# Modulation rows by column-tiled TensorE products, and two side steps per place in the hybrid stage

## What is computed

```python
def adaln(c, w, b):
    mod = jax.nn.silu(c) @ w + b                 # c: 1 x 1024, w: 1024 x 3072
    shift, scale, gate = jnp.split(mod[:, None, :], 3, axis=-1)
    return shift, scale, gate

def modulate(x, norm_w, shift, scale):
    return rmsnorm(x, norm_w) * (1 + scale) + shift

# for each of hyb, dense, ssm, moe:
shift, scale, gate = adaln(c, mod_w, mod_b)
x = x + gate * stage(modulate(x, norm, shift, scale))
```

## Time and profile before

| | |
|---|---|
| median of three runs | 2512.43 us (2510.99 to 2514.09) |
| the profiled execution, its own time | 2508.9 us |
| its span, first to last instruction | 2507.1 us |
| mean granted TensorE clock | 0.977 |
| busy: TensorE, VectorE, ScalarE, GpSimd | 94%, 79%, 58%, 9% |

### The profile page before, as it was taken

How to read it: one execution, slowest core, us unless ns; L and a number is a source line. 1 busy time by engine, 2 the same in 40 slices (tenths; PEclk the granted TensorE clock), 3 DMA queues, 4 the chain that set the end, 5 groups by cost and what they waited for, 6 DMA issues and landing times.

```text
span 2507.1 us, 33025 instructions
## 1 busy us (share of the span) xinstructions
PE 2365.5 (94%) x13939; PEld 2069.0 (83%) x13939; DVE 1976.4 (79%) x2135; ACT 1460.5 (58%) x1679; POOL 218.5 (9%) x271
## 2 busy tenths in 40 slices
PE   5898999899989999999999999998999999899998
PEld 4776998798778888888888888887888997887997
DVE  5857876799678989898999898986667865767875
ACT  3344433467557777777777777774555654445562
POOL 1100111101000000000000000001401211320110
PEclk8998999999989999999999999999999999999999
DMA  9754777544559999999999999995124554223551
GB/s 319 243 200 142 246 278 285 194 152 168 196 191 361 351 359 352 360 353 359 348 360 357 354 359 345 365 339 187 68 101 151 202 192 158 99 75 119 209 211 68
DMA packets 264887, 612.71 MB, mean 244 GB/s; under 512 B 18696, under 2 KB 33370, under 8 KB 264730
## 3 DMA queue, kind: packets, MB, share of 16 engines
q1 hardware_dynamic: 247824, 554.39, 61.5%
q0 software_dynamic: 15824, 55.72, 6.6%
q10 hardware_dynamic: 1082, 0.40, 0.1%
HBM read 609.40 MB, written 1.08 MB: 244 GB/s over the span
## 4 chain that ended last, share of the span: by engine, by line
PE 72%; DVE 14%; DMA 6%; ACT 5%; issue 2%; POOL 1%; SPq 0%; DVEq 0%; ACTq 0%; POOLq 0%
PE ps L132 70%; PE ps L136 2%; DMA slots<-in_moe_w_gu 2%; DVE ul_moe_w L145 2%; DVE macc L153 1%; DVE eb L145 1%; ACT uh_moe_w L139 1%; DVE gate L153 1%; DMA beside<-in_moe_mod_w 1%; DVE ul_ssm_w L145 1%; DMA slots<-in_hyb_mod_w 1%; ACT xn L139 1%; DMA beside<-in_dense_mod_w 1%; DVE xn L150 1%; DVE xn L153 0%
## 5 line engine op out<-in xcount | busy, mean ns | idle before, releaser
L145 DVE TENSOR_TENSOR ul_moe_w<-slots,uh_moe_w 128x2048 fp32r<-128x2048 f32 x334 | 761.0, 2290 | 93.7 <-ACT uh_moe_w L139 92.9
L139 ACT ACTIVATE uh_moe_w<-slots 128x2048 fp32r<-128x2048 f32 x334 | 639.5, 1917 | 203.7 <-PE ps L132 156.1
L132 PE MATMUL ps<-uh_moe_w,XGh 128*128 128x512 f32 x896 | 354.9, 396 | 4.2 <-DVE XGl L145 2.1
L132 PE MATMUL ps<-uh_moe_w,XGl 128*128 128x512 f32 x896 | 349.6, 390 | 0.0
L132 PE MATMUL ps<-ul_moe_w,XGh 128*128 128x512 f32 x896 | 349.0, 390 | 0.0
L145 DVE TENSOR_TENSOR ul_ffn<-slots,uh_ffn 128x2048 fp32r<-128x2048 f32 x64 | 145.8, 2291 | 79.3 <-ACT uh_ffn L139 79.3
L132 PEld LDWEIGHTS ps<-uh_moe_w,XGh 128*128 128x128 f32 x896 | 168.3, 188 | 42.2 <-DVE ul_moe_w L145 6.8
L132 PE MATMUL ps<-HTf,uh_ffn 128*128 128x256 f32 x704 | 199.4, 283 | 2.0 <-DVE HTlf L145 2.0
L132 PE MATMUL ps<-HTf,ul_ffn 128*128 128x256 f32 x704 | 199.2, 283 | 0.0
L132 PE MATMUL ps<-HTlf,uh_ffn 128*128 128x256 f32 x704 | 199.2, 283 | 0.0
L132 PEld LDWEIGHTS ps<-uh_moe_w,XGl 128*128 128x128 f32 x896 | 168.2, 188 | 36.0
(11 more groups left out here) (530 smaller groups left out, 5510.0 us busy)
## 6 DMA issues: line engine op xcount, KB each, us to landing
slots<-in_moe_w_gu SPq DMA_DIRECT2D x111, 2048.0 KB, 9.5
slots<-in_moe_w_down SPq DMA_DIRECT2D x56, 2048.0 KB, 8.7
slots<-in_w_up SPq DMA_DIRECT2D x20, 2048.0 KB, 8.0
slots<-in_w_in SPq DMA_DIRECT2D x14, 2048.0 KB, 8.7
slots<-in_dense_w_gu SPq DMA_DIRECT2D x10, 2048.0 KB, 11.1
slots<-in_ssm_w_in SPq DMA_DIRECT2D x10, 2048.0 KB, 8.7
slots<-in_w_down SPq DMA_DIRECT2D x10, 2048.0 KB, 8.4
slots<-in_dense_w_down SPq DMA_DIRECT2D x5, 2048.0 KB, 11.1
```

Source lines behind the costliest of these rows:

```text
L132: return self.e.matmul(o, lhsT, rhs, start=start, stop=stop, skip_group_check=skip) if self.e else DONE
L139: return self.e.activation(o, i, f, **kw) if self.e else DONE
L145: return self.e.tensor_tensor(o, a, b, op) if self.e else DONE
```

## The change

Six parts (hybrid 2, dense 0 to 2, ssm 0 and 1) are no longer accumulated by VectorE. For every chunk TensorE makes four float32 products: the 128 numbers of silu(c), repeated to 32 columns, are the stationary operand; the moving operand is one quarter of the chunk's columns (256); quarter i goes to the partitions 32i to 32i+31 of one PSUM bank, accumulated over the eight chunks. It is now the TensorE product that frees the buffer. After the eighth chunk VectorE copies 128 x 256 to `macc`; for shift and scale TensorE transposes it in two pieces and VectorE adds the bias from every 32nd column; for the gate TensorE makes four products with one repeated column of the identity. A part of columns now costs 12 steps and a part of rows 13.

In the hybrid stage the steps are doubled from unit `V` (the ninth) on, in the attention and beside the output projection; at its end both engines run on until ssm's shift and scale are done (before: hybrid's gate). ssm 2 and moe 0 to 2, with 32 chunks, are left for the dense stage and stay on VectorE; its pace becomes (3, 4). The pools of banks change so that bank 3 belongs to the side work alone.

```diff
+    def steps(self, n):
+        for _ in range(n):
+            self.step()
...
+BY_TENSOR = {("hyb", 2), ("dense", 0), ("dense", 1), ("dense", 2), ("ssm", 0), ("ssm", 1)}
...
-                free[n % 3] = side.v.at((name, n))
+                free[n % 3] = (side.t if (name, part) in BY_TENSOR else side.v).at((name, n))
                 if k == KC - 1:
+                    if (name, part) in BY_TENSOR:
+                        yield
+                        yield
...
+    def spread_done(e, name, part):
+
+        s1, s2 = s12[name]
+        s_ = (s1 if part else s2)[:, :].rearrange("p (b a) -> p a b", a=2)
+        ps = c.psum.of(("mod", name, part))
+        e.wait_ge(*side.t.at(("mod", name, part)))
+        e.wait_ge(*S.v.at(("cols", "m")))
+        e.tensor_tensor(s_, ps.t[:, 0:256].rearrange("p (a b q) -> p b a q", a=2, q=32)[:, :, :, 0],
+                        vec[name + "_mod_b"][:, part * 8:part * 8 + 8].rearrange("p (b a) -> p b a", a=2), ALU.add).then_inc(*side.v.up(("mod", name, part)))
...
+    def spread_tensor(e, name, part, k, n, x):
+
+        if k == 0:
+            ps = c.side_banks.take(("spread", name, part))
+            e.wait_ge(*ps.was)
+        ps = c.psum.of(("spread", name, part))
+        e.wait_ge(*S.v.at("sc"))
+        e.wait_ge(*beside_landed[n % 3].at((name, n)))
+        for i in range(4):
+            m = e.matmul(ps.t[32 * i:32 * i + 32, 0:256], sc[:, k:k + 1].to_broadcast([128, 32]), x[:, 256 * i:256 * (i + 1)], k == 0, k == KC - 1)
+        m.then_inc(*side.t.up((name, n)))
+
+    def spread_turned_tensor(e, name, part):
...
+        for a in range(2):
+            m = e.transpose(ps.t[:, a * 128:(a + 1) * 128], macc[:, a * 128:(a + 1) * 128], K["ident"])
+        m.then_inc(*side.t.up(("mod", name, part)))
+
+    def spread_row_tensor(e, name, part, i):
...
+        for b in range(2):
+            r = 32 * (2 * i + b)
+            m = e.matmul(ps.t[:, b * 256:(b + 1) * 256], K["ident"][:, r:r + 1].to_broadcast([128, 128]), macc[:, 0:256])
+        m.then_inc(*side.t.up(("gate", name, i)))
...
     def side_vector(e, me):
...
+                if (name, part) in BY_TENSOR:
+                    if k < KC - 1:
+                        continue
+                    yield
+                    ps = c.psum.of(("spread", name, part))
+                    e.wait_ge(*side.t.at((name, n)))
+                    e.wait_ge(*last)
+                    e.tensor_copy(macc[:, 0:256], ps.t[:, 0:256]).then_inc(*side.v.up(("spread", name, part)))
+                    c.psum.leave(("spread", name, part), side.v)
+                    for _ in range(3):
+                        yield
+                    if part < 2:
+                        last = spread_done(e, name, part)
+                    else:
+                        gate_done(e, name, slot, (0,))
+                        yield
+                        last = gate_done(e, name, slot, (1,))
...
-    bk1, bk2, bs = c.pool(range(3)), c.pool([4, 3]), c.pool([3])
-    bkb, bt = [c.pool([5, 6, 7]), c.pool([0, 1, 2])], c.pool([0, 1])
+    bk1, bk2, bs, bv = c.pool(range(3)), c.pool([4, 5]), c.pool([3]), c.pool([6, 7])
+    bkb, bt = [c.pool([6, 7, 5]), c.pool([0, 1, 2])], c.pool([0, 1])
...
     def tile_tensor(e, n):
-        c.side_t.step()
+        c.side_t.steps(2 if n >= V else 1)
...
     def tile_vector(e, n):
-        c.side_v.step()
+        c.side_v.steps(2 if n >= V else 1)
...
     def out_after(e, n):
         if n == 2:
             mix_tensor(e, range(4, 8))
+        c.side_t.step()
...
         c.side_banks = c.banks
-        c.side_t.until(("hyb", "rows"))
+        c.side_t.until(("ssm", ("cols", 1)))
         S.t.mark("end")
...
-        c.side_v.until(("hyb", "rows"))
+        c.side_v.steps(3)
+        c.side_v.until(("ssm", ("cols", 1)))
         c.lead("hyb_out")
...
-        c.side_t.pace = (1, 1)
+        c.side_t.pace = (3, 4)
...
-        c.side_v.pace = (1, 1)
+        c.side_v.pace = (3, 4)
```

More of the change, by code:

```diff
@@ L988, in side_gpsimd, with gate_done @@
                     me.done.add((name, "rows" if part == 2 else ("cols", part)))
+    def gate_done(e, name, slot, halves=(0, 1)):
+        for i in halves:
+            ps = c.psum.of(("gate", name, i))
+            g = gates[slot][:, i * 512:(i + 1) * 512]
+            e.wait_ge(*side.t.at(("gate", name, i)))
+            e.wait_ge(*bias_landed[name].at("bias"))
+            e.tensor_tensor(g, g, ps.t[:, :], ALU.add).then_inc(*side.v.up(("gate", name)))
+            c.psum.leave(("gate", name, i), side.v)
+        return side.t.at(("gate", name, 1))
@@ L1014, in side_vector @@
                     continue
[L1015 to L1022, removed]
+                last = gate_done(e, name, slot)
                 me.done.add((name, "rows"))
@@ L1030, in side_tensor @@
                 yield
+                if (name, part) in BY_TENSOR:
+                    spread_tensor(e, name, part, k, n, bufs[n % 3])
+                    if k < KC - 1:
+                        continue
+                    for _ in range(3):
+                        yield
+                    if part < 2:
+                        spread_turned_tensor(e, name, part)
+                    else:
+                        spread_row_tensor(e, name, part, 0)
+                        yield
+                        spread_row_tensor(e, name, part, 1)
+                    yield
+                    me.done.add((name, "rows" if part == 2 else ("cols", part)))
+                    continue
                 if k < KC - 1:
@@ L1770, in attention_tensor @@
         hidden_tensor(e, 1)
-        c.side_t.step()
+        c.side_t.steps(2)
         turn_tensor_heads(e, 0, 1, 4)
@@ L1842, in attention_vector @@
         gated_heads_vector(e)
-        c.side_v.step()
+        c.side_v.steps(2)
         compressed_vector(e)
-        c.side_v.step()
+        c.side_v.steps(2)
         O.split_lo(e, 0)
@@ L1947, in vector @@
         O.split_lo(e, 3)
-        c.side_v.step()
+        c.side_v.steps(2)
         O.split_lo(e, 4)
-        c.side_v.step()
+        c.side_v.steps(2)
         mix_vector(e, range(4, 8))
         for n in range(5, 8):
-            c.side_v.step()
+            c.side_v.steps(2)
             O.split_lo(e, n)
-        for _ in range(2):
-            c.side_v.step()
-        c.side_v.until(("hyb", "rows"))
+        c.side_v.steps(3)
+        c.side_v.until(("ssm", ("cols", 1)))
         c.lead("hyb_out")
```

28 lines of the change are left out of this document (22 added, 6 removed).

## The result

The kernel takes 2523.55 us after the change (median of six runs, 2519.18 to 2529.08) and 2513.26 us before it (median of six runs, 2510.84 to 2518.43): ratio 1.0036, 95% interval 1.0023 to 1.0048. It is slower by 0.36%, some 9 us; 2519 was forecast. The profiled execution of after took 2529.08 us, the longest of its six, 5.5 us above their median. (The kernel's line of `spread_done` that makes `s_` rearranges to `p b a`, where the diff above has `p a b`.)

The account below looks back on a forecast made before the run. TensorE, busy 94% of the span, was taken to bound the dense stage; +2.6 +9.4 -1.7 +13.5 -17.3 = +6.5 us gave 2515.4 for the profiled execution, 2519 for the median, range 2498 to 2540.

Parts of the forecast that it names:

- A small loss: Whole kernel: likeliest case, +2 to +14 us, 2513 to 2527 us, chance 0.32.
- Chunk cost: TensorE, each chunk's four products: 0.65 us if column groups overlap, 31 us for 48 chunks.
- The two upper bounds: Chunk on TensorE: 1.0 us if only two groups overlap (chance 0.09), 1.86 if none do (0.02).
- Tiles: Hybrid stage, 84 to 161 us: 23 chunks +15.0, savings, load waits +5 (bounds 0 and 12); sum +9.4 us.
- The wait of 3.85 us for `hyb_pe`: Tiles, before dense 0's column sum: TensorE's wait for bank 3, held by VectorE for a copy, goes.
- Attention: 161 to 217 us: five chunks +3.3, partly hidden, VectorE relieved; sum -1.7 us, bounds +3.3 and -13.
- The half clock between 192 and 212 us: Attention: TensorE's clock of 0.56 there; its disappearance was named as a sign of being wrong, bound -13 us.
- End of the hybrid stage: 217 us to first dense tile: 13 chunks on TensorE, late loads, serial chain; +13.5 us, bounds +7 and +20.
- Dense stage: Column sums of ssm and TensorE's waits go, VectorE's 16 fewer chunks count nothing; -17.3 us, bounds -10 and -24.
- VectorE was the releaser: Rival, hybrid stage: VectorE held TensorE up and gets faster; -12.5 us, 2500 us, chance 0.31.
- The waits for chunks decide: Rival, hybrid stage: tiles wait 12 us and the end costs 20; +13.5 us, 2532 us, chance 0.09.
- They cancel: Rival, whole kernel: dense stage gives back 24 us, the rest stays; 2512 us, chance 0.17.

Follow-up runs that it names:

- b3: The change with all four products of a chunk in one column group, the six parts' values mixed up; 2549.59 us, ratio 1.0149.
- b4: The change with only two of each chunk's four products, the rest of the six parts' sums left out; 2518.32 us, ratio 1.0025.
- a4: The change with products reading the identity instead of chunks, so TensorE waits for no chunk load; six parts' values left out; 2505.76 us, ratio 0.9976.
- a2: The kernel before with hybrid 2 and dense 0 to 2 as TensorE products, single steps and pace (1, 1) kept; 2530.49 us, ratio 1.0079.
- a1: The change with all ten parts on VectorE, so only doubled steps and slower pace against the kernel before; 2542.02 us, ratio 1.0121.
- b1: The change with a fourth chunk buffer for hybrid 2 and dense 0 to 2, ssm keeping three; 2513.51 us, ratio 1.0003.
- c4: The change with four buffers, five parts on TensorE, and VectorE's five hybrid-end ssm chunks made behind the dense stage's first rows; 2513.23 us, ratio 1.0003.
- a3: The change with both engines stopping at dense's rows, the rest of ssm done in the dense stage with bank 3 kept; 2524.31 us, ratio 1.0047.

## Why the prediction came out as it did

**Direction and size.** A small loss was the likeliest case, with +6.5 us on the profiled execution; the ratio gives +9. The time fell into that case's own range (2513 to 2527). Part of this agreement is luck. In the traces the hybrid stage lost 40.2 us where the terms add up to 23.8, and the dense stage gave back 22.6 where 17.3 were forecast: the loss and the gain were both taken too small. From trace to trace the whole is +20.2 us and not +6.5; it is the medians that lie 10 us apart. (The terms meet at 84, 161 and 217 us of the trace of before and the landmarks lie a little elsewhere, so each term is compared only roughly.)

**Chunk cost: right.** 0.65 us was taken, 0.67 read with the change of form, 0.46 where two stand in a row. The two upper bounds are out: a chunk in one group costs 1.85 us (b3), and four products in four groups last no longer than two in two (b4). The Trainium skill (TensorEngine Tiling (Array Packing), Key Properties) has a change of mode drain TensorE; the trace agrees in that the next product starts 0.23 us later instead of 0.12, 0.1 us per visit. The estimate made from the Trainium skill (TensorE: Matmul & The Clock Gate, Part 3), 0.59 us, lay as near to these readings as mine.

**Tiles: the step that was mis-sized.** "I take 1 us at four or five places: +5." The attention began 17.8 us later in the trace of after, where the terms up to 161 us come to 12 (to 19 with the upper bound of the waits). Without waits for loads it begins at 148.8, only 3.4 us later than before, so that between these two executions, the slowest of after and the fastest of a4, the waits and what follows them are 14.4 us of the 17.8; in the medians they are 15 to 18 us over the whole hybrid stage. TensorE's waits themselves are 6.4 us before the attention, near the 5, and 12.9 in all, above the 10 that the prediction named as a sign of being wrong. What was mis-sized is what hangs on them. One part is that the wait closes a ring (product, release, load, product), so that one late load makes the next one late. The other is the clock, 0.91 instead of 0.96 in that window; the prediction had counted on a gain of 1.7 us there. How the 14.4 us divide between the two isn't shown. The loads were longer too, 6.4 us instead of 4.4, but a4 has them at 6.3 and doesn't lose by it. The wait of 3.85 us for `hyb_pe` went as predicted, and the window from 122 to 134 us is at full clock.

**Attention.** -1.7 predicted, +4.1 read. The half clock between 192 and 212 us is gone (0.91), as the prediction feared for itself; but it came back at another place, 0.54 between 226 and 234 us. That relief of VectorE does shorten this stretch, a2 shows with its single steps: 65.6 us. With doubled steps it takes 71.2 without load waits (a4) and 74.2 with them. Why the doubled steps cost 5.6 us isn't settled by a run of its own.

**End of the hybrid stage.** +13.5 predicted, +18.3 read (first dense tile at 296.8 instead of about 280; 5 of the 17 us arise here, the rest before the projection). The sequence was right step by step: last load, last product, copy, transposes, bias, low part, gated rows. The load was taken at 6.3 us and took 9.15. The same end without load waits is 53.4 us instead of 59.4, so two thirds of the 18.3 stay when no load is waited for.

**Dense stage: -17.3 predicted, -22.6 read,** inside its bounds. All the stops of TensorE that were listed are gone or hidden: no releaser stands in the chain for 193.68 us, the wait at 458 has vanished, and the last gate sum of moe starts at 471.39, 19 us before the stage's last rows begin at 490.5 (20 were predicted). I had left 3.6 us of moe's waits and 1.9 us of its last part in the sum; that no wait is left in the chain fits the 5.3 us that were missing. That VectorE's 16 chunks count nothing there was right; what counts is that TensorE has no column sum to wait for, as a1 shows with all parts on VectorE and the same 203.5.

**The rivals.** "VectorE was the releaser" was too strong: relieved of its chunks at single steps, the kernel reaches the projection 1.7 us earlier (213.8), not 14; the attention alone is 4.5 us shorter. But VectorE can't take the doubled steps (a1). "The waits for chunks decide" had the right mechanism and would have been the better forecast for the hybrid stage (37.3 us against 23.8; 40.2 read); the dense stage paid 5 us of it back. "They cancel" is the time of the change with the fourth buffer.

**Where the 22.6 us go.** Each attempt to keep the dense stage's gain and lose less in the hybrid stage ended between 2512 and 2524 us, or far above. The chunks have to pass by somewhere: at the hybrid end they hold up rows (after, a1, b1), in the dense stage they hold up sums (before, c4; in a3 the single bank as well). Of the kernels that compute everything, only the buffer paid, in both arrangements.

## What to carry to other kernels

An engine that executes in order should read a prefetched buffer only if the time between the buffer's release and its next use is longer than the load as it is in the new kernel (here 6.4 us in the median and 9.15 in the chain, not the 4.4 of the kernel before); count uses per microsecond where they are densest, not on the average. Moving a cheap consumer to the bounding engine moves its waits there as well, and they cost it idle time and clock; so give it depth first, and measure what the depth alone brings to the old kernel. Don't place side work whose result is needed late ahead of the rows that the next stage needs first.

## What was not expected of the hardware

- One wait of 4.49 us was followed by 20 us at the lower of TensorE's two clocks (1.2 GHz, granted 0.50), in which the same 32 products took 7.09 us instead of 3.79. TensorE was busy for 19.57 of those 20 us. By the estimate above, what followed the wait cost twice the wait. It is one pair of traces.
- Two float32 products in two column groups, standing alone, take as long as four in four groups (0.56 us), while the four in one group take 1.85.
- A chunk that another chunk follows takes 0.46 us from start to start, one that another form of product follows 0.56.
- The loads of 512 KB into `beside` took 4.4 us in the median before and 6.4 after between 60 and 240 us, though the rate was lower (257 and 228 GB/s between 84 and 161 us). No run shows why.
